# Nine modulation sums in one run on GpSimd, and a norm that waits for the ninth

## What is computed

```python
# first block, its end
f = rmsnorm(h, norm_ff_w)
h = h + jnp.square(jax.nn.relu(f @ w_ff1)) @ w_ff2      # d_ff 4096, "first feed-forward"
x = rmsnorm(h, final_norm_w)
# second block
mods = jnp.split(jax.nn.silu(c) @ w_ada + b_ada, 9, axis=-1)     # w_ada: 1024 x 9216
sh1, sc1, gt1, sh2, sc2, gt2, sh3, sc3, gt3 = mods
u = rmsnorm_2(x, g_ff1) * (1 + sc1) + sh1
h = x + 0.5 * gt1 * swiglu(u, w1_gate, w1_up, w1_down)  # d_ff 2816, "second feed-forward"
u = rmsnorm_2(h, g_mix) * (1 + sc2) + sh2               # attention and mLSTM follow, with gt2
...                                                     # then a third feed-forward with sh3, sc3, gt3
```

## Time and profile before

| | us |
|---|---|
| Median of 3 runs | 2008.24 (2007.74 to 2013.01) |
| The profiled execution | 2008.84 |
| Its span in the trace | 2006.8 |
| PE busy in the span | 1963.7 |
| DVE busy | 1144.3 |
| ACT busy | 785.8 |
| GpSimd busy | 365.9 |
| Mean granted clock of PE, share of 2.4 GHz | 0.996 |

### The profile page before, as it was taken

How to read it: one execution, slowest core, us unless ns; L and a number is a source line. 1 busy time by engine, 2 the same in 40 slices (tenths; PEclk the granted TensorE clock), 3 DMA queues, 4 the chain that set the end, 5 groups by cost and what they waited for, 6 DMA issues and landing times.

```text
span 2006.8 us, 25581 instructions
## 1 busy us (share of the span) xinstructions
PE 1963.7 (98%) x9558; PEld 1576.2 (79%) x9558; DVE 1144.3 (57%) x1762; ACT 785.8 (39%) x1330; POOL 365.9 (18%) x298
## 2 busy tenths in 40 slices
PE   8999999999999999999999999999999999999998
PEld 6876678888887788888888977777677788888887
DVE  7576667777667655453564266665634755444444
ACT  7436433222225222222332345557756342222223
POOL 3000039999200695000000000000000000000000
PEclk9999999999999999999999999999999999999999
DMA  6320146666332664323245433334126423233331
GB/s 167 90 65 27 53 141 204 201 199 209 124 94 73 178 198 138 102 86 105 84 128 131 121 119 108 105 95 132 57 79 202 118 74 105 84 105 91 97 99 58
DMA packets 274990, 233.13 MB, mean 116 GB/s; under 512 B 16631, under 2 KB 248442, under 8 KB 274368
## 3 DMA queue, kind: packets, MB, share of 16 engines
q1 hardware_dynamic: 255792, 166.29, 28.5%
q0 software_dynamic: 17488, 60.36, 9.7%
q10 hardware_dynamic: 1632, 5.45, 1.2%
HBM read 214.95 MB, written 12.58 MB: 113 GB/s over the span
## 4 chain that ended last, share of the span: by engine, by line
PE 91%; DVE 4%; ACT 2%; issue 1%; DMA 1%; ACTq 0%; SPq 0%; DVEq 0%; POOLq 0%
PE bank L1138 25%; PE bank L1140 25%; PE bank L1139 25%; PE bank L1144 2%; PE bank L1145 2%; PE bank L1686 1%; PE bank L1703 1%; PE bank L1586 1%; PE bank L1831 1%; PE bank L1848 1%; PE bank L1355 1%; DVE wlo L1933 1%; PE bank L1194 1%; PE bank L1507 1%; PE bank L1403 1%
## 5 line engine op out<-in xcount | busy, mean ns | idle before, releaser
L1138 PE MATMUL bank<-xhi,whi 128*128 128x512 f32 x1680 | 666.9, 397 | 5.1 <-PE bank L1703 2.1
L1140 PE MATMUL bank<-xhi,wlo 128*128 128x512 f32 x1680 | 656.5, 391 | 0.0
L1139 PE MATMUL bank<-xlo,whi 128*128 128x512 f32 x1680 | 655.5, 390 | 0.0
L1933 DVE TENSOR_TENSOR wlo<-stage,whi 128x1024 fp32r<-128x1024 f32 x309 | 407.1, 1329 | 208.2 <-ACT whi L564 207.9
L564 ACT ACTIVATE whi<-stage 128x1024 fp32r<-128x1024 f32 x309 | 321.1, 1051 | 406.2 <-PE bank L1140 363.4
L1138 PEld LDWEIGHTS bank<-xhi,whi 128*128 128x128 f32 x1680 | 316.0, 188 | 76.2 <-issue 9.7
L1140 PEld LDWEIGHTS bank<-xhi,wlo 128*128 128x128 f32 x1680 | 315.9, 188 | 67.7
L1139 PEld LDWEIGHTS bank<-xlo,whi 128*128 128x128 f32 x1680 | 316.4, 188 | 63.1
L2324 DVE SCALAR_TENSOR_TENSOR H<-bank,sc,H 128x512 f32<-128x512 f32 x304 | 217.8, 746 | 77.3 <-PE bank L1140 75.5
L1138 PE MATMUL bank<-hidhi,whi 128*128 128x512 f32 x532 | 209.8, 394 | 0.0
L1140 PE MATMUL bank<-hidhi,wlo 128*128 128x512 f32 x532 | 208.5, 392 | 0.0
(11 more groups left out here) (447 smaller groups left out, 2079.2 us busy)
## 6 DMA issues: line engine op xcount, KB each, us to landing
arena<-in_w_ada POOLq DMA_DIRECT2D x72, 512.0 KB, 4.0
stage<-in_w_in SPq DMA_DIRECT2D x71, 512.0 KB, 3.9
stage<-in_w_ff SPq DMA_DIRECT2D x64, 512.0 KB, 4.2
stage<-in_w_gate SPq DMA_DIRECT2D x44, 512.0 KB, 4.5
stage<-in_w_up SPq DMA_DIRECT2D x44, 512.0 KB, 3.8
stage<-in_w_down SPq DMA_DIRECT2D x44, 512.0 KB, 3.9
arena<-arena ACTq DMA_DIRECT2D x16, 256.0 KB, 5.6
stage<-in_w_proj_a SPq DMA_DIRECT2D x8, 512.0 KB, 4.1
```

What stands on the lines that cost most here:

```text
L1138: mm(out, sh, mh, start=start, stop=False, **kw)
L1139: mm(out, sh, ml, start=False, stop=False, **kw)
L1140: return mm(out, sl, mh, start=False, stop=stop, **kw)
L1933: V.tensor_tensor(wlo[:, static % SPLITS, :], stage[:, static % STAGES, :], whi[:, static % SPLITS, :].bitcast(F32), ALU.subtract).then_in ...
```

## The change

Two places of the semaphore plan. GpSimd no longer waits at unit 48: it goes on from the sixth sum to the seventh, and makes all nine in one run. ACT waits for `ada_acc` of 9 where it waited for 6, ahead of everything it does for norm 3. The tiles are the same, so are all instructions and their order on each engine.

```diff
@@ ScalarE, norm(k)
             def norm(k, first=0):
                 if k == 3:
-                    act.wait_ge(s("ada_acc"), 6)
+                    act.wait_ge(s("ada_acc"), 9)
                 e = eps[:, 2:3] if k == 3 else eps[:, 0:1] if norm_eps[k] == EPS1 else eps[:, 1:2]
@@ GpSimd, loop over the 72 units
             for n in range(total):
                 m, kt = divmod(n, KT)
-                if n == 6 * KT:
-                    pool.wait_ge(s("mods_out"), 2)
                 if n + 2 < total:
                     load(n + 2)
```

## The result

| | before | changed |
|---|---|---|
| Median, us (6 runs each) | 2008.77 (2007.19 to 2013.01) | 2020.27 (2016.53 to 2027.00) |
| Ratio | | 1.0053, 95% interval 1.0036 to 1.0070 |
| The profiled execution | 2008.84 | 2016.53 |
| Its span | 2006.8 | 2014.5 |
| Mean granted clock, profiled execution | 0.996 | 0.995 |

The change makes the kernel slower by half a per cent. The forecast was 2018.4 with a range of 2014.3 to 2023.5. The profiled execution is the fastest of its six; the experiments show that it owes this to what lies ahead of 280 us, and that the change costs as much in it as in a longer one.

What follows compares the result with a forecast made beforehand. PE was taken to bound the kernel, busy 1963.7 of 2006.8 us. From 2008.84: + 9.9 (squares) + 1.5 (clock) - 1.8 (second feed-forward) + 0 (first) gave 2018.4 us, range 2014.3 to 2023.5.

Steps and rivals of the forecast that it cites:

- The ninth sum: GpSimd, running on after the sixth sum's COPY at 514.95, has the ninth ready at 627.6 us, bounds 625.9 to 631.3.
- What the wait costs: Norm 3: ACT's squares start 10.4 us later, and through DVE's sums PE's L1222 comes later, + 9.9 us, bounds 8.2 to 13.6.
- PE's two idle times: Norm 3: PE stands still about 6 us ahead of L1608 and about 2.5 us ahead of L1222.
- The clock: PE falls to 1.2 GHz around its norm 3 waits: + 1.5 us, between 0 and 3.4.
- Rival B: PE keeps 1.2 GHz through norm 3's products, some 14 us, losing up to 7: 2024 us; chance 0.08.
- The second feed-forward: Its first groups run without GpSimd's 24 units beside them: gain 1.8 us, between 1.6 and 2.0.
- The first feed-forward: Its further five groups overlap GpSimd: about 0.6 us, covered by PE's later wait, so 0 in the sum.
- Rival A: Ninth sum ready at about 616, before the squares at 617.52: 2007.0 to 2007.7 us, no change; chance 0.04.

Runs made afterwards that it cites:

- a1: The changed kernel run again with nothing altered: median 2021.81 us beside 2009.61 for the kernel before, 54.71 us across norm 3.
- e4: Kernel before with GpSimd's pause after the eighth sum instead of the sixth, two plain squares' tiles moved: 2009.14 us beside 2009.89 for the kernel before.
- e2: Changed kernel with the ninth sum's arithmetic left out but for its first unit, loads kept: 2011.60 us beside 2009.61 for the kernel before.
- e7: The same kernel as e2, run again: 2009.86 us beside 2010.49 for the kernel before.
- e5: Changed kernel with only four plain squares, moved behind ACT's root, waiting for the ninth sum: 2014.39 us beside 2009.89 for the kernel before.

## Why the prediction was right, step by step

The time, its sign and the chain were right. By its steps:

- **The ninth sum.** Predicted 112.6 us after the sixth COPY; measured 113.0 (39.1, 38.4 and 35.5 for the three sums). The tail behind 616 did run faster, as expected. In the trace the end stands at 626.15, not 627.6, because the sixth sum lies 1.8 us earlier in it, with all of the first feed-forward.
- **What the wait costs.** Predicted + 9.9; across norm 3 it is + 9.58, or 10.2 with the 0.59 by which norm 3's start was later. Behind L1586 the squares start 10.05 us later than before, and L1222 9.48 later, since a slack is used up. The prediction had the right chain but misread that slack: it took 0.4 us, from DVE's last sum. By the rows above PE waits for the last weighted square first, and that slack was 0.59. ACT's sixteen squares, DVE's ladder and everything behind kept their distances (626.30 to 635.71 for the squares, 9.4 as before), as the prediction said.
- **PE's two idle times.** Predicted 6 and 2.5, measured 6.60 and 1.32. The second is shorter since L1608 ran at half the clock and took 1.27 us of it; without that it would be 2.6.
- **The clock.** Predicted 1.5 with bounds of 0 and 3.4. The three traces have 0, 1.7 and 0. The fall came in each of them, and mostly lay within the wait. The term was too large by about a us, within its bounds. Rival B (the clock staying low through the products) was seen in none of the three. What the prediction drew from the Trainium skill ("TensorE: Matmul & The Clock Gate", HAM oscillation — how this bites in real kernels), that the fall is certain here, came true in all three traces. The price of 1.8 to 3.4 that it set on the fall, from its own rows, did not: no trace has it, a1 with 1.7 comes near.
- **The second feed-forward.** Predicted - 1.8, measured - 1.55; the 0.2 for its first group wasn't there (34.63 against 34.61).
- **The first feed-forward.** Predicted + 0.6 and covered; measured + 0.59. Covered is right, since GpSimd and not PE sets when norm 3 starts, but the distance of norm 3 is taken from a later start, so by the distances the sum is 0.59 + 9.58 - 1.55 = 8.6, against 9.9 - 1.8 = 8.1 without the clock. The 0.59 isn't spread over the groups, as the 22.06 of the prediction has it: three of the four intervals take 21.93 or 21.94, as before, and the last one 22.52. e4, where GpSimd stops after the eighth sum, has 87.73 as before.
- **Rival A.** The ninth sum did not come in time. e2 and e7 show what would have been: norm 3 as before, and medians within noise of the kernel before.

The trace gives 8.6 us and the profiled execution is 7.7 longer than that of before. That the median lies nearer 11 above than 8 isn't explained by a term of the sum; it was inside the range. So it is in part luck that 2018.4 lies within 2 us of 2020.27: the clock term was larger than what norm 3 showed, and it stood in for a us or so that the runs added from places that no term of the sum names.

## What to carry to other kernels

Before a wait is moved to a later count, read when that count is reached and what stands in each queue behind the waiting instruction: here a wait of ACT held DVE for 9.9 us, and through DVE's fourth add and ACT's last weighted square it held PE for 7.9. Work on a side engine is free only up to the moment when someone needs it, so the last piece that still fits (eight sums, not nine) is the place to stop. And narrowing a wait to the tiles that need it can bring the side engine's work beside a chain of two-operand instructions of DVE, which it slows.

## What the runs showed of the hardware

- DVE and GpSimd held each other up where DVE's instruction had both inputs in SBUF: a DVE sum of 128x512 took 0.68 us alone and up to 2.24 us beside GpSimd, and GpSimd's add of 128x1024 2.42 and up to 3.28. DVE's adds with one input in PSUM kept their 0.74 beside it. I had counted this for GpSimd's pace only, and not for DVE's chain in e5.
- In e5 this made the ladder of squares and sums, 9.1 us long before, one of 13.2.
- A fall of PE's clock to half inside a wait cost nothing by itself: L1608 took 2.79 us instead of 1.52 and was still done before its successor was due. Where the low stretch lay behind the wait, it cost: 1.7 us of 3.4 in a1, 2.8 of 6.8 in e5.
- The runs of the kernel before spread over 2006 to 2019 us, and go with the mean granted clock (0.997 to 0.991). The low stretches lie in different places from one execution to the next, in parts of the program that are the same: the first L1586 of the feed-forwards came between 280.8 and 289.7 us in the 14 traces.
